# Sum of squares of a new residual: gathered by GpSimd during the output projection instead of taken from the new x, at two block ends

## The reference, cut to what matters

```
h = retention(rms_norm(x, a_norm_pre[i]), a_w_in[i], a_w_out[i])
x = x + rms_norm(h, a_norm_post[i])
...
h = diff_attention(rms_norm(x, b_norm_pre[i]), k_sh, v_sh, b_w_q[i], ...)
x = x + rms_norm(h, b_norm_post[i])
...
h = conv_ffn(rms_norm(x, ffn_norm_pre[layer]), ffn_w_up[layer], ...)
```

## Time and profile before

| | us |
|---|---|
| median of three runs (lowest to highest) | 2843.84 (2843.55 to 2844.67) |
| the profiled execution, its own time | 2845.79 |
| its span in the trace | 2844.0 |
| PE busy in the span | 2763.0 (97%) |
| DVE busy | 1621.1 (57%) |
| ACT busy | 1191.2 (42%) |
| POOL busy | 180.1 (6%) |

### The profile page before, as it was taken

The page is one execution under the profiler, slowest core; times in us unless marked ns, Lnnn a source line. Parts: engine busy times, 40 slices in busy tenths (PEclk is TensorE's granted clock), DMA queues, the critical chain, the costliest instruction groups (busy, mean ns, idle before and its releaser), DMA issues.

```text
span 2844.0 us, 34173 instructions
## 1 busy us (share of the span) xinstructions
PE 2763.0 (97%) x11820; PEld 2087.0 (73%) x11820; DVE 1621.1 (57%) x2230; ACT 1191.2 (42%) x1922; POOL 180.1 (6%) x208
## 2 busy tenths in 40 slices
PE   8999999999999989999999999999988999999999
PEld 6777776888877656888876667888866555788887
DVE  4444436777245765777338975554366666555532
ACT  4333334444234544444326754333234666433321
POOL 0000000000000000000004810000000333000000
PEclk9999999999999999999999999999999999999999
DMA  4222232333322112333331213333333100233333
GB/s 146 74 74 75 81 89 68 95 96 94 90 82 89 52 37 68 96 95 94 90 96 45 60 54 95 95 89 92 94 96 106 31 16 23 79 92 95 96 89 96
DMA packets 421251, 229.34 MB, mean 81 GB/s; under 512 B 8035, under 2 KB 413612, under 8 KB 421036
## 3 DMA queue, kind: packets, MB, share of 16 engines
q1 hardware_dynamic: 418700, 224.39, 27.0%
q10 hardware_dynamic: 2464, 3.81, 0.4%
HBM read 226.07 MB, written 2.10 MB: 80 GB/s over the span
## 4 chain that ended last, share of the span: by engine, by line
PE 85%; DVE 7%; ACT 4%; issue 2%; POOL 1%; DMA 0%; ACTq 0%; DVEq 0%; POOLq 0%
PE lin L779 22%; PE lin L781 22%; PE lin L780 22%; PE att L1060 1%; PE lin L1112 1%; PE att L944 1%; DVE w_both L2085 1%; PE att L909 1%; PE att L907 1%; PE att L908 1%; PE stat L801 1%; POOL con_p L740 1%; ACT w_both L1458 1%; PE lin L1100 1%; PE trp L1077 1%
## 5 line engine op out<-in xcount | busy, mean ns | idle before, releaser
L2085 DVE TENSOR_TENSOR w_both<-raw,w_both 128x1024 fp32r<-128x1024 f32 x427 | 525.0, 1229 | 571.2 <-ACT w_both L1458 557.0
L779 PE MATMUL lin<-xh,w_both 128*128 128x512 f32 x1856 | 741.0, 399 | 8.2 <-DVE w_both L2085 7.9
L780 PE MATMUL lin<-xl,w_both 128*128 128x512 f32 x1856 | 733.3, 395 | 0.0
L781 PE MATMUL lin<-xh,w_both 128*128 128x512 f32 x1856 | 733.3, 395 | 0.0
L1458 ACT ACTIVATE w_both<-raw 128x1024 fp32r<-128x1024 f32 x427 | 452.2, 1059 | 659.4 <-PE lin L781 575.4
L779 PEld LDWEIGHTS lin<-xh,w_both 128*128 128x128 f32 x1856 | 348.2, 188 | 102.9 <-issue 15.3
L780 PEld LDWEIGHTS lin<-xl,w_both 128*128 128x128 f32 x1856 | 348.2, 188 | 86.3 <-issue 2.9
L781 PEld LDWEIGHTS lin<-xh,w_both 128*128 128x128 f32 x1856 | 348.0, 188 | 85.0
L779 PE MATMUL lin<-ffn_hi,w_both 128*128 128x512 f32 x704 | 280.0, 398 | 0.0
L781 PE MATMUL lin<-ffn_hi,w_both 128*128 128x512 f32 x704 | 279.1, 396 | 0.0
L780 PE MATMUL lin<-ffn_lo,w_both 128*128 128x512 f32 x704 | 279.1, 396 | 0.0
(11 more groups left out here) (408 smaller groups left out, 3807.0 us busy)
## 6 DMA issues: line engine op xcount, KB each, us to landing
raw<-in_ffn_w_up SPq DMA_DIRECT2D x176, 512.0 KB, 3.8
raw<-in_ffn_w_down SPq DMA_DIRECT2D x64, 512.0 KB, 3.9
raw<-in_a_w_in SPq DMA_DIRECT2D x48, 512.0 KB, 3.8
raw<-in_ffn_w_down SPq DMA_DIRECT2D x32, 384.0 KB, 3.4
raw<-in_conv_w_pw SPq DMA_DIRECT2D x24, 512.0 KB, 4.0
raw<-in_nsa_w_in SPq DMA_DIRECT2D x21, 512.0 KB, 3.7
raw<-in_a_w_out SPq DMA_DIRECT2D x16, 512.0 KB, 4.0
raw<-in_w_kv SPq DMA_DIRECT2D x16, 512.0 KB, 3.9
```

Source lines behind the costliest of these rows:

```text
L779: pe.matmul(bank, w_hi[s][:, k, :], h, start=start and k == 0, stop=False)
L780: pe.matmul(bank, w_hi[s][:, k, :], l, start=False, stop=False)
L781: done = pe.matmul(bank, w_lo[s][:, k, :], h, start=False, stop=stop and k == kc - 1)
L2085: dve.tensor_tensor(w_lo[s][:, :, :], raw[s][:, :, :], w_hi[s][:, :, :].bitcast(F32), ALU.subtract).then_inc(lo_done[s], 1)
```

## The change

At the two block ends that a conv FFN follows directly (retention and attention), the sum of squares of the new `x` is no longer taken from the new `x`. With g the gained `h`, sum (x + g*rs)^2 = sum x^2 + 2*rs*sum(x*g) + rs^2*sum(g^2).

- ACT copies `h` with the gain (`gained_out`), signals `gh_ready`, and frees the bank only after the weight split behind it.
- POOL, during the projection: for chunks 0 to 6 `x*g` and `g*g`, and their running sums (2 instructions for chunk 0, 4 for each later one, all tensor_tensor of 128x512 in SBUF).
- PE: `occupy` goes there; two ones-matmuls on POOL's sums, after a wait for all of them, and two on the products of chunk 7, after a wait for those (`gh_last`): one made by ACT (square of g, behind the copy of chunk 7), one by DVE (x*g, behind `xl` of chunk 0). The eight `sum_square` in `beside` go.
- DVE waits for POOL's sums before its first update; `y` becomes a tensor_tensor `hT*rs`.
- ACT squares no new `x` there; it copies the two sums out of PSUM, behind `xh` of chunks 1 and 2; POOL then makes the new sum in `x_sum` with four dependent instructions, and ACT takes `rs_x` from it behind `xh` of chunk 7.
- `x_sum` first gets a copy of `stat` by ACT (`total_of_x`) early in retention and again early in attention.
- `POOL_Y` is empty: all eight updates stay on DVE. A few semaphores are merged to make room (`start_in`, `tables_in`, `r_rot`); the waits on them count on.

```diff
+POOL_Y = ()
+GH_STEPS = 2 + 6 * 4 + 4
...
+            def closing(hT, gh, nth, turned):
+                own, last_, sums = gh[:, 0:2, :], gh[:, 2:4, :], gh[:, 4:6, :]
+                ghs.next()
+                for c in range(DC - 1):
+                    pool.wait_ge(gh_ready, ghs.next())
+                    if c == 0:
+                        pool.tensor_tensor(sums[:, 0, :], hT[:, c, :], x[:, c, :], ALU.mult).then_inc(gh_step, 1)
+                        pool.tensor_tensor(sums[:, 1, :], hT[:, c, :], hT[:, c, :], ALU.mult).then_inc(gh_step, 1)
...
+                        continue
+                    pool.wait_ge(gh_step, steps.last())
+                    pool.tensor_tensor(own[:, 0, :], hT[:, c, :], x[:, c, :], ALU.mult).then_inc(gh_step, 1)
+                    pool.tensor_tensor(own[:, 1, :], hT[:, c, :], hT[:, c, :], ALU.mult).then_inc(gh_step, 1)
+                    for k in range(2):
+                        pool.wait_ge(gh_step, steps.next())
+                        pool.tensor_tensor(sums[:, k, :], sums[:, k, :], own[:, k, :], ALU.add).then_inc(gh_step, 1)
...
+                ghs.next()
+                pool.wait_ge(gh_ready, ghs.next())
+                pool.tensor_tensor(own[:, 0, :], sums[:, 1, :], rs[:, :], ALU.mult).then_inc(gh_step, 1)
+                pool.wait_ge(gh_step, steps.next())
+                pool.tensor_tensor(own[:, 1, :], own[:, 0, :], sums[:, 0, :], ALU.add).then_inc(gh_step, 1)
+                pool.wait_ge(gh_step, steps.next())
+                pool.tensor_tensor(own[:, 0, :], own[:, 1, :], rs[:, :], ALU.mult).then_inc(gh_step, 1)
+                pool.wait_ge(gh_step, steps.next())
+                pool.tensor_tensor(x_sum[:, :], x_sum[:, :], own[:, 0, :], ALU.add).then_inc(gh_step, 1)
...
@@ PE, closed()
-                occupy(att[:, 0, :], 4)
+                if late is None:
+                    occupy(att[:, 0, :], 4)
+                    return
+                nth = closings.next()
+                pe.wait_ge(gh_step, nth * GH_STEPS - 4)
+                for k in range(2):
+                    pe.matmul(att[:, 1 + k, :], c_("ones"), late[:, 4 + k, :], start=True, stop=False)
+                pe.wait_ge(gh_last, 2 * nth)
+                for k in range(2):
+                    pe.matmul(att[:, 1 + k, :], c_("ones"), late[:, 2 + k, :], start=False, stop=True).then_inc(gh_sum, 1)
@@ PE, ffn()
-                    beside(xh, xl, lambda k: (xl_ready, first_ + k + 1), LAG, True)
+                    beside(xh, xl, lambda k: (xl_ready, first_ + k + 1), LAG)
@@ ACT, project_out()
+                def gained_out(k, b):
+                    act.activation(hT[:, at(k), :], lin[b][:, :], ACT.Copy, scale=col(gains[0], k + gains[1])).then_inc(gh_ready, 1)
+                def released(b):
+                    act.wait_ge(gh_ready, ghs.next())
+                    act.sem_inc(bank_free[b], 1)
...
+                if gh is not None:
+                    nth = closings.next()
+                    act.activation(gh[:, 3, :], hT[:, DC - 1, :], ACT.Square).then_inc(gh_last, 1)
                 if then is not None:
                     for c in range(DC):
-                        gained_x(c, (upd.n + 1) * DC + c + 1, *then, dst=acc if summed and c == 0 else None)
+                        gained_x(c, (upd.n + 1) * DC + c + 1, *then, dst=acc if summed and c == 0 else None, squared=gh is None)
+                        if gh is not None and 1 <= c <= 2:
+                            act.wait_ge(gh_sum, 2 * nth - 2 + c)
+                            act.activation(gh[:, 3 + c, :], att[:, c, :], ACT.Copy, scale=2.0 if c == 1 else 1.0).then_inc(gh_ready, 1)
+                            ghs.next()
...
+            def total_of_x():
+                act.activation(x_sum[:, :], stat[:, :], ACT.Copy).then_inc(gh_ready, 1)
+                ghs.next()
@@ ACT, ffn()
-                    act.wait_ge(sq_used, squares.last())
+                    act.wait_ge(gh_step, closings.last() * GH_STEPS)
+                    inverse_rms(D, x_sum, dst=rs_x)
@@ DVE, project_out()
+                if gh is not None:
+                    dve.wait_ge(gh_step, closings.next() * GH_STEPS - 4)
...
+                    if gh is None:
+                        dve.scalar_tensor_tensor(y[c % 2][:, :], hT[:, c, :], col(gain, g0 + c), rs[:, :], ALU.mult, ALU.mult).then_inc(t_ready, 1)
+                    else:
+                        dve.tensor_tensor(y[c % 2][:, :], hT[:, c, :], rs[:, :], ALU.mult).then_inc(t_ready, 1)
...
+                    if gh is not None and c == 0:
+                        dve.wait_ge(h_ready, closes.last() + 1)
+                        dve.tensor_tensor(gh[:, 2, :], hT[:, DC - 1, :], x[:, DC - 1, :], ALU.mult).then_inc(gh_last, 1)
```

More of the change, by code:

```diff
@@ L301, in program @@
         att_lo = m.place("att_lo", [P, AH, T], F32R)
-        dif_hT = Map(m.at).place("dif_hT", [P, DC, T])
+        m2 = Map(m.at)
+        dif_hT = m2.place("dif_hT", [P, DC, T])
+        dif_gh = m2.place("dif_gh", [P, 6, T])
         xqh = m.place("xqh", [P, DC, T], F32R)
@@ L724, in _ @@
                 elsewhere(upd)
+                closing(dif_hT, dif_gh, 1 + run[0] + run[1], (run[0] + run[1]) * DC)
             if run[3]:
@@ L1482, in gained_x, with project_out @@
                 pre.next()
-                square(x[:, at(c), :], apart=not isinstance(c, int), dst=dst)
-            def project_out(hT, nu, final=False, then=None, first=0, between=(), table=True, normed=False, summed=False):
+                if squared:
+                    square(x[:, at(c), :], apart=not isinstance(c, int), dst=dst)
+            def project_out(hT, nu, final=False, then=None, first=0, between=(), table=True, normed=False, summed=False, gains=None, gh=None):
                 if table:
@@ L1508, in project_out @@
                     square(lin[b][:, :])
-                    act.activation(hT[:, o, :], lin[b][:, :], ACT.Copy).then_inc(bank_free[b], 1)
-                with rounds(act, (DC - first) // 2 - 1, (units, 2 * nu), (banks, 2), (squares, 2)) as i:
+                    gained_out(o, b)
+                    released(b)
+                counted = () if gh is None else ((ghs, 2),)
+                with rounds(act, (DC - first) // 2 - 1, (units, 2 * nu), (banks, 2), (squares, 2), *counted) as i:
                     for o in range(2):
@@ L1606, in retention @@
                         act.sem_inc(rms_known, 1)
+                        total_of_x()
                         act.preload_act_table_set(SILU)
@@ L2113, in add_square, with project_out @@
                 dve.tensor_tensor(acc[:, :], acc[:, :], sq[(squares.n - 1) % 2][:, :], ALU.add).then_inc(sq_used, 1)
-            def project_out(hT, nu, gain, g0, final=False, then=None, first=0, between=(), summed=False, normed=None):
+            def project_out(hT, nu, gain, g0, final=False, then=None, first=0, between=(), summed=False, normed=None, gh=None):
                 dve.memset(acc[:, :], 0.0).then_inc(acc_zero, 1)
@@ L2139, in project_out @@
                 dve.wait_ge(rs_ready, rss.next())
+                if gh is not None:
+                    dve.wait_ge(gh_step, closings.next() * GH_STEPS - 4)
                 def update(c):
                     n = upd_t.next()
+                    if gh is not None and c in POOL_Y:
+                        return
                     if n > 2:
@@ L2153, in low @@
                     lower_x(c, *then)
-                    if not summed:
+                    if gh is not None:
+                        pass
+                    elif not summed:
                         squares.next()
@@ L2232, in rotate @@
                         done = dve.tensor_tensor(dst[:, half, :], ret_m[:, 0, :], ret_m[:, 1, :], op)
-                        done.then_inc(r_rot if half else rot_half, 1)
-                    dve.wait_ge(r_rot, n + 1)
+                        done.then_inc(r_rot, 1)
+                    dve.wait_ge(r_rot, 2 * (n + 1))
                 def gate(h, c):
@@ L2380, in nsa @@
                         with_positions(n, pair)
-                dve.wait_ge(n_tab_in, 16)
+                dve.wait_ge(tables_in, 16 * (2 * run[0] + 1))
                 for i in range(4):
```

87 lines of the change are left out of this document (53 added, 34 removed).

## The result

The changed kernel takes 2850.14 us at the median of 20 runs (2846.82 to 2853.33), the kernel before 2844.07 (20 runs, 2842.25 to 2851.03). The ratio is 1.0019, 95% interval 1.0013 to 1.0026: +5.4 us (3.7 to 7.4). Forecast were +9.2 us, 2853.0; the range was 2838 to 2860, the forecast's own part of it 2849 to 2857.

A forecast was written before the change was run, and what follows sets the result against it. PE, busy 97% of the span, was taken to bound the kernel, with DVE close below at the end. Retention +1.2, attention +1.2 + 5.3 and clock +1.5 gave +9.2 us, 2853.0; range 2838 to 2860.

The forecast's parts named there:

- Step 1: Both block ends: PE's eight sums in `beside` go and DVE sets the pace, without collisions; -3.2 us an end.
- Step 2: Both ends: POOL's last four instructions stretch DVE's chain by 4.4 us; with the sums' gain, +1.2 us an end.
- step 4: Both ends: PE idles, its clock falls to 0.50 and matmuls run slow; 0.75 us an end, +1.5 us.
- Step 3: Attention's projection: POOL's chunk sums fall behind and DVE's first `y` waits for them; +5.3 us, once.
- the sign that I gave: Retention's end: PE's clock at 0.5 about 450 would show the forecast right.
- Rival A: Both ends: POOL's last four do not collide with DVE's chain; 2837.4 to 2839 us, chance 0.22.
- B: Attention: POOL's sums are done by 1101.5, the last four still collide; 2846 to 2848 us, chance 0.22.
- C: Both ends: PE stays at 1.2 GHz through both `beside`; +17.7 us, 2861.5 us, chance 0.11.

The follow-up runs named there:

- e3: Changed kernel without POOL's last four instructions at each end and without its g*g products of chunks 1 to 6 and their additions in attention: 2838.39 us.
- e1: Changed kernel without POOL's last four instructions at each block end: 2840.04 us, -4.3 us against the kernel before.
- e9: Changed kernel with POOL's last four instructions made to wait for the last `xl`, nothing left out: 2851.22 us, +9.1 us against the kernel before.
- e6: Changed kernel with the last four operations on DVE, from PSUM behind its last `xl`, nothing left out: 2846.51 us, +2.3 us against the kernel before.
- e2: Changed kernel without POOL's g*g products of chunks 1 to 6 and their additions in attention: 2846.71 us, +1.4 us against the kernel before.
- e7: Changed kernel with the squares of g made by ACT in attention's projection, nothing left out: 2846.85 us, +2.8 us against the kernel before.
- e10: e8 with the first of DVE's last four operations put ahead of its last `xl`: 2841.88 us, ratio 0.9994 against the kernel before.
- e4: The change at retention's end alone, attention's end as in the kernel before: 2846.05 us, +1.1 us against the kernel before.
- e8: Changed kernel with the edits of e6 and e7 together, nothing left out: 2843.95 us, ratio 0.9994 against the kernel before.
- e5: Changed kernel with dummy matmuls on PE in the block ends' gaps, issued at two later places too: 2854.07 us, +9.7 us against the kernel before.

## Why the prediction came out as it did

**Step 1 right.** It forecast, without collisions, the last `xl` at 461.6, the next output at 466.3 and -3.2 us an end. e3 is that case: moved to the same T (0.37 us later) it has 461.54 and 466.32, and -3.16 and -3.17.

**Step 2 right in mechanism and nearly in size.** The four stretched DVE instructions carry 1.01, 1.09, 0.94 and 1.01 us more, 4.05, where I had 4 x 1.1 = 4.4 from the earlier trace rows. e1 takes the instructions away, e9 moves them, e6 gives them to DVE: each time 16.5 us come back, so this is shown. Step 1 with 4.06 and 0.29 for the clock gives -3.16 + 4.06 + 0.29 = +1.19; measured +1.20. That the forecast for step 2 was +1.2 too is luck to the hundredth: it had 0.34 too much for the stretch and nothing for the clock, and with step 4's 0.75 this end was forecast at +1.95. By the rule of the Trainium skill (SBUF — State Buffer, "Who interferes with whom") whoever starts first holds the pair while the other waits. The trace agrees: each meeting delays one DVE instruction by 0.94 to 1.09 us, and POOL's by 0.3 to 0.4 (1.59 to 1.71, 1.29 alone in e9). That DVE loses less than POOL's 1.29 does not speak against the rule. Take from each row's end the time that it needs alone: by this estimate each DVE instruction starts 0.07 to 0.20 us after POOL's got going, and gets going itself 0.13 to 0.20 before POOL's recorded end.

**Step 3 right in mechanism, mis-sized: +5.3 forecast, +3.1 measured.** (From `rs` to the first `y` 3.78 us for 0.66; e2 and e7 bring 0.66 back.) I had chunk 2 begin at 1074.5 and it began at 1072.95, in an execution that runs 0.23 us later there: "chunks 0 and 1 cost it 11 us" were 9.6. From there on I had 32.2 us to the end and it was 31.9. So 1.8 of the 2.2 us are the first two chunks. One reason can be read off: the product of a tile with itself takes POOL 1.04 us where DVE does not hold it up (1075.01 above), and I had put in the 1.24 to 1.41 of the earlier trace rows for all four.

**Step 4 too large: +1.5 forecast, +0.3 measured.** In retention the sign that I gave, 0.5 about 450, did not come: PE idles from 444.7 to 448.2 and the clock stays at 1.00. It falls to 0.50 only at 456.6, in the stretched part, and is back at 463.4. In attention it falls twice: before PE's first chunk, as forecast (0.50 from 1101.7 to 1108), and again in the stretched part (0.50 from 1116 to 1122). All these cold matmuls lie in time that DVE sets, but for retention's 0.3. The size of 0.75 is not impossible: e2's 5.52 at retention is 0.74 above 4.78, with matmuls 0.43 us apart up to 467.4 and the last `xl` at 467.61. Over these runs the cost goes with where the return to 2.4 GHz falls against the last `xl`.

**The sum.** Of the +9.2 forecast, 5.2 came at the ends: 2.2 us less in step 3, 1.2 in step 4, 0.7 in step 2. The mechanism of each step but the clock's timing was right; the three sizes all erred to the same side, which put the time at the low edge of the forecast's own range. Rival A (no collision) falls with the 1.75 us rows, B (POOL keeps up) with the `y` at 1104.90, C (PE at 1.2 GHz through both `beside`) with the clock at 1.00 from 465 in retention and from 1123 in attention. Had step 3 been at 0 as in B, the ends would be those of e7, +2.1 us (its time: +2.8), where B had +2.4 and +4 with the clock.

## What to carry to other kernels

Work moved from the busy engine to an idle one is not free if the idle one is GpSimd and VectorE is next in line to be the pace: here each GpSimd instruction beside VectorE's chain cost the chain 1.0 us, more than VectorE needs (0.69) to do the same instruction itself. So count meetings, not only GpSimd's own time, and ask whether the helper keeps up with the rate at which work comes. And when the effect is a few us in some thousands, compare the one stretch from marker to marker in the profiles: there it showed to 0.1 us, in the times only to 2 or 3. Keep the whole time as the control even so: in the profiles of e6 and e10 some 2 us of what the ends gained were lost behind them.

## What the runs showed of the hardware that I had not expected

- GpSimd's tensor_tensor of 128x512 takes 1.04 us when both inputs are the same tile (`dif_hT` by itself, 1075.01 above), and 1.27 to 1.31 with two, where DVE does not hold it up. The two operations are both products, so it is not the operation that differs.
- POOL's four instructions in a row and DVE's chain take turns one by one where they meet, DVE at 1.63 to 1.77 and POOL at 1.59 to 1.71 each.
- What the clock does behind the same gap differs from profile to profile. In the seventh block, whose code all these kernels share, PE idles 2.8 us and soon afterwards 4.15 us in the changed kernel, 2.8 and 3.90 in e6. In the changed kernel the clock stays at 1.00 behind the first gap (2120) and falls only at the end of the second, at 2125.7; in e6 it falls already at 2116, before the second gap, and reads 0.50 all through it. Timelines of PE there, first the changed kernel, then e6:

```profile
2125.86 2.08 PE L1014 MATMUL att<-sq,const 128*128 128x512 f32 x2 [4.15 <-ACT sq L1521]
...
2128.59 0.63 PE L827 MATMUL lin<-xh,w_both 128*128 128x512 f32 x1
2129.01 0.43 PE L825 MATMUL lin<-xh,w_both 128*128 128x512 f32 x1
```

```profile
2120.86 2.07 PE L1006 MATMUL att<-sq,const 128*128 128x512 f32 x2 [3.90 <-ACT sq L1513]
...
2125.72 0.63 PE L818 MATMUL lin<-xl,w_both 128*128 128x512 f32 x1
2126.15 0.56 PE L819 MATMUL lin<-xh,w_both 128*128 128x512 f32 x1
```

  The last slow matmul starts 3.2 us behind the gap in the one and 5.3 in the other, and e6 is 1.1 us later from there on. At 2194 it happens again: behind a gap of 1.87 to 1.89 us, the same in all twelve profiles, the clock falls to 0.50 for some 3 us in e4, e6, e8 and e10, which are 1.5 us later from there on, and stays at 1.00 in the other eight.
  From attention's next output to the program's end e6, e8 and e10 need 1720.3, 1719.4 and 1720.1 us, all the others but e5 1716.8 to 1718.7, the last being e4. In the profiled executions that is where e6, e8 and e10 lose some of what their ends gain. It can't belong to VectorE's making the last four operations alone, since in e4 GpSimd makes them and the clock falls behind the same gap at 2194. What decides it I can't say: I found no instruction that differs there, and the question stays open.
